# Attention of both layers: query rotation in two halves, per-head normalisation, ScalarE's high parts placed elsewhere, and the first tile's dense output products behind all groups

## The reference, cut to what matters

```python
q = (rmsnorm(cq, g_q[l]) @ w_uq[l]).reshape(B, S, 8, 64 + 32)
q_nope, q_rope = q[..., :64], apply_rope(q[..., 64:], cos_r, sin_r)   # the rotation
kv = (rmsnorm(ckv, g_kv[l]) @ w_ukv[l]).reshape(B, S, 8, 64 + 64)
o_a = mla_attention(q_nope, q_rope, k_nope, k_rope, v_mla)            # softmax, 8 heads
o_b = dsa_attention(...)                                              # 4 heads, 64 of the keys
o_c = silu(rg) * head_groupnorm(retention(...))
x = x + concatenate([o_a, o_b, o_c], axis=-1) @ w_out[l]              # dense output
hf = rmsnorm(x, g_mlp[l])
x = x + square(relu(hf @ w_ff1[l])) @ w_ff2[l]
```

## Time and profile before

| what | value |
|---|---|
| median of 3 runs | 1395.91 us (1393.72 to 1396.88) |
| profiled execution | 1395.43 us |
| its span | 1393.4 us |
| PE busy | 1347.1 us, 97% of the span |
| DVE, ACT, POOL busy | 622.7, 541.0, 449.3 us |
| TensorE clock | 9 in all 40 slices (full speed) |

### The profile page before, as it was taken

One profiled execution on the slowest core, in us unless ns is written; L12 is line 12 of the kernel. 1 busy time (PEld: TensorE's weight loads), 2 busy tenths in 40 slices (PEclk: granted clock), 3 DMA queues, 4 the chain that ended last, 5 costly groups with the idle time before them and its releaser, 6 DMA issues.

```text
span 1393.4 us, 19892 instructions
## 1 busy us (share of the span) xinstructions
PE 1347.1 (97%) x7754; PEld 931.0 (67%) x7754; DVE 622.7 (45%) x1060; ACT 541.0 (39%) x790; POOL 449.3 (32%) x295
## 2 busy tenths in 40 slices
PE   8998999999999999999999999999999999999998
PEld 7786788887887788888887877755434444344343
DVE  5685554544687455353344887523202112122021
ACT  6667644435576654343555562212111111111011
POOL 2384454444374544543867913000000000000000
PEclk9999999999999999999999999999999999999999
DMA  7441454553533355455786351479999999999997
GB/s 289 137 168 67 152 181 181 185 202 127 207 116 110 116 204 190 181 182 181 237 278 225 103 208 52 137 290 411 422 428 428 427 428 428 428 427 427 428 423 292
DMA packets 50250, 351.99 MB, mean 253 GB/s; under 512 B 7747, under 2 KB 9679, under 8 KB 25583
## 3 DMA queue, kind: packets, MB, share of 16 engines
q1 hardware_dynamic: 49438, 349.52, 64.9%
q10 hardware_dynamic: 720, 1.20, 0.2%
HBM read 347.78 MB, written 1.07 MB: 250 GB/s over the span
## 4 chain that ended last, share of the span: by engine, by line
PE 72%; DMA 11%; DVE 7%; ACT 3%; issue 3%; DVEq 2%; POOL 1%; SPq 0%; ACTq 0%; POOLq 0%
PE psum L1925 12%; PE psum L1101 9%; PE psum L1103 9%; PE psum L1102 9%; PE psum L1396 9%; DMA ring<-in_w_expert_up 8%; PE psum L1946 5%; PE psum L1398 4%; PE psum L1091 4%; PE psum L1853 2%; POOL weights_split L908 1%; PE psum L1863 1%; DMA arena<-in_w_expert_down 1%; DVE arena L2577 1%; ACT weights_split L2040 1%
## 5 line engine op out<-in xcount | busy, mean ns | idle before, releaser
L908 POOL TENSOR_TENSOR weights_split<-weights_raw,weights_split 128x512 fp32r<-128x512 f32 (+2 forms) x253 | 401.6, 1621 | 338.2 <-ACT weights_split L2040 338.2
L2040 ACT ACTIVATE weights_split<-weights_raw 128x2048 fp32r<-128x2048 f32 (+4 forms) x154 | 243.5, 1586 | 243.5 <-PE psum L1103 145.3
L1925 PE MATMUL psum<-ring,arena 128*64 128x512 f32 x944 | 226.5, 598 | 12.1 <-DMA ring<-in_w_expert_up 11.2
L1396 PE MATMUL psum<-h_split,weights_split 128*128 128x512 f32 x512 | 182.1, 399 | 3.1 <-DVE h_split L2028 2.7
L1925 PEld LDWEIGHTS psum<-ring,arena 128*64 128x64 f32 x944 | 73.4, 138 | 136.4 <-issue 135.8
L1101 PE MATMUL psum<-weights_split,h_split 128*128 128x512 f32 (+3 forms) x400 | 151.9, 380 | 4.3 <-POOL weights_split L908 2.4
L1101 PE MATMUL psum<-weights_split,hidden_split 128*128 128x512 f32 (+1 forms) x384 | 151.1, 393 | 4.3 <-DVE hidden_split L2028 4.3
L908 DVE TENSOR_TENSOR weights_split<-weights_raw,weights_split 128x2048 fp32r<-128x2048 f32 (+3 forms) x53 | 119.3, 2257 | 70.1 <-ACT weights_split L2040 68.3
L1102 PE MATMUL psum<-weights_split,h_split 128*128 128x512 f32 (+3 forms) x400 | 149.5, 374 | 0.0
L1103 PE MATMUL psum<-weights_split,h_split 128*128 128x512 f32 (+3 forms) x400 | 149.2, 373 | 0.0
L1103 PE MATMUL psum<-weights_split,hidden_split 128*128 128x512 f32 (+1 forms) x384 | 147.3, 384 | 0.0
(11 more groups left out here) (379 smaller groups left out, 1734.5 us busy)
## 6 DMA issues: line engine op xcount, KB each, us to landing
weights_raw<-in_layer_w SPq DMA_DIRECT2D x94, 1024.0 KB, 4.8
arena<-in_w_expert_down SPq DMA_DIRECT2D x28, 2048.0 KB, 14.7
ring<-in_w_expert_up SPq DMA_DIRECT2D x28, 2048.0 KB, 15.0
ring<-in_w_expert_gate SPq DMA_DIRECT2D x23, 2048.0 KB, 16.2
weights_raw<-in_second_w SPq DMA_DIRECT2D x44, 512.0 KB, 4.7
arena<-in_w_expert_gate SPq DMA_DIRECT2D x4, 2048.0 KB, 10.2
ring<-in_w_expert_up SPq DMA_DIRECT2D x8, 1024.0 KB, 13.1
arena<-in_w_expert_down SPq DMA_DIRECT2D x16, 512.0 KB, 12.3
```

The source lines that it names most:

```text
L908: ins = eng.tensor_tensor(W.part(j, 1, n)[:, cols], W.raw(j, n)[:, cols], W.part(j, 0, n).bitcast(F32)[:, cols], ALU.subtract)
L1396: pe.matmul(both.rearrange("p (w s) -> p w s", w=2), w[0][:, k, f * P:(f + 1) * P], hTp[:, :, k, :], start=(k == 0), stop=False)
L1925: ins = pe.matmul(bank[half(j), :], xe[h][:, k, half(j)], w[j][:, k, :], start=(k == 0), stop=(k == KD - 1))
L2040: act.activation(W.part(j, 0, w), W.raw(j, w), ACT.Copy).then_inc(W.hi, 1)
```

## The change

Four edits, in both layers.

1. VectorE rotates the queries in two calls, heads 0 to 3 behind `norm_probs(1)` and heads 4 to 7 behind `norm_probs(3)`, in place of one call behind `low_values(0)`. `low_values(0)` now stands behind them.
2. `norm_probs` multiplies head by head with `tensor_scalar` (two instructions for a group of two heads, four for one of four) in place of one `tensor_tensor` with a broadcast factor.
3. ScalarE makes the high part of out(1,1) in front of `exponentials(2)`, was behind the turned keys; that of out(0,0) behind the square root of the retention's variance, was behind `empty_turned(4)`; that of ff1(0,0) behind `high_values(7)`, was behind `high_values(6)`.
4. PE's dense output products: the chunks 4 and 5 come first and the wait for mixT stands in front of chunks 6 and 7; out(1,1) of tile 1 is cut in two, behind `turn_probs(7)` and `turn_probs(8)`; all products of piece out(0,0) and out(1,0) stand behind `attend_values(9)`. `add_out` follows them.

```diff
-                units.wait_emptied(("O", 0), ("mixT", 3))
-                project_out(0, 1, 0, range(4))
+                units.wait_emptied(("O", 0))
+                project_out(0, 1, 0, (0, 1))
                 units.wait_emptied(("O", 2))
-                project_out(0, 1, 1, range(4), True)
+                project_out(0, 1, 1, (0, 1))
+                units.wait_emptied(("mixT", 3))
+                project_out(0, 1, 0, (2, 3))
+                project_out(0, 1, 1, (2, 3), True)
...
                 attend_values(5)
-                project_out(1, 1, 1, range(4), True)
                 attend_mla(8)
                 turn_probs(7)
+                project_out(1, 1, 1, (0, 1))
                 attend_values(6)
+                attend_mla(9)
+                turn_probs(8)
+                project_out(1, 1, 1, (2, 3), True)
+                attend_values(7)
                 units.wait_emptied(("O", 4), ("O", 5))
-                project_out(0, 0, 0, (0, 1))
-                attend_mla(9)
-                project_out(0, 0, 0, (2, 3))
-                turn_probs(8)
-                attend_values(7)
-                project_out(1, 0, 0, range(4))
                 turn_probs(9)
                 attend_values(8)
+                attend_values(9)
+                project_out(0, 0, 0, range(4))
                 units.wait_emptied(("O", 6), ("O", 7))
                 project_out(0, 0, 1, (0, 1))
-                attend_values(9)
...
+                units.wait_emptied(("O", 8), ("O", 9))
+                project_out(0, 0, 1, (2, 3))
+                project_out(1, 0, 0, range(4))
                 units.wait_emptied(("wout", 0), ("wout", 1))
                 transposes(pe, units, "tr3", x, (0, 1))
-                project_out(1, 0, 1, (2, 3))
+                project_out(1, 0, 1, range(4))
...
                 empty_q(1)
+                split_after("uq", 0, 2)
                 exponentials(2)
...
                 act.activation(ret_rstd, ret_var, ACT.Sqrt, bias=eps_c, scale=1.0 / RET_E).then_inc(ret_std_ready.sem, 1)
+                split_after("ukv", 0, 0)
                 high_values(2)
...
                 high_values(7)
+                split_after("out", 1, 1)
                 empty_turned(9)
...
-                    rows = scores[g % 2][:, 0:n * nk].rearrange("p (h k) -> p h k", h=n)
-                    dve.tensor_tensor(rows, rows, rinv[g % 3][:, 0:n].unsqueeze(2).to_broadcast([P, n, nk]), ALU.mult).then_inc(probs_normed.sem, 1)
+                    for j in range(n):
+                        rows = scores[g % 2][:, j * nk:(j + 1) * nk]
+                        ins = dve.tensor_scalar(rows, rows, rinv[g % 3][:, j:j + 1], None, ALU.mult)
+                    ins.then_inc(probs_normed.sem, 1)
+
+                def rotate_queries(c):
+                    units.wait_emptied(("uq", T * c), ("uq", T * c + 1))
+                    return rotate(dve, *halves(q[:, :, 4 * c:4 * c + 4, NOPE:QK]), *angles(ROPE), q_tmp)
...
                 norm_probs(1)
+                rotate_queries(0)
...
                 norm_probs(3)
+                rotate_queries(1).then_inc(q_roped.sem, 1)
                 low_values(0)
-                units.wait_emptied(*(("uq", j) for j in range(2 * T)))
-                rotate(dve, *halves(q[:, :, :, NOPE:QK]), *angles(ROPE), q_tmp).then_inc(q_roped.sem, 1)
```

More of the change, by code:

```diff
@@ L344, in layer_plan @@
     plan += [scores[4], scores[5], ("mixT", 3, 7, "V"), turned[4], scores[6], turned[5], values[4], scores[7], turned[6], values[5], scores[8], turned[7], values[6], scores[9]]
-    plan += [wout[0], turned[8], values[7], wout[2], turned[9], values[8], values[9], wout[1]] + turned_x[:2] + [wout[3]] + turned_x[2:]
+    plan += [turned[8], values[7], turned[9], values[8], values[9], wout[0], wout[1], wout[2]] + turned_x[:2] + [wout[3]] + turned_x[2:]
     for b in range(FFB):
@@ L2180, in _ @@
                         dst, bank[0:NOPE, :].rearrange("p (c s) -> p c s", c=4), ACT.Copy), "A")
-                split_after("uq", 0, 2)
                 mix_gain = lambda k: gain(G_RET)(k - (KD - 2)) if k >= KD - 2 else None
@@ L2186, in _ @@
                 empty_turned(4)
-                split_after("ukv", 0, 0)
                 empty_turned(5)
@@ L2197, in _ @@
                 high_values(6)
-                split_after("out", 1, 1)
                 empty_turned(8)
@@ L2730, in _ @@
                 mask_scores(9)
-                add_out(0)
                 low_values(7)
                 norm_probs(9)
-                add_out(2)
                 low_values(8)
                 low_values(9)
+                add_out(0)
                 add_out(1)
+                add_out(2)
                 low_transposed(dve, units, "tr3", 2, gain(G_MLP), hTp, hT_hi, l, (0, 1), 1)
```

## The result

The changed kernel takes 1411.34 us (median of 3 runs, 1408.67 to 1412.46) against 1395.91: a ratio of 1.0108, 95% interval 1.0085 to 1.0131. It is slower, and by more than the forecast range allowed. The profiled execution took 1408.67 us, 13.2 more than that of before, and its span is 1406.6 us. In that trace the last feed-forward matmul of layer 0 starts 5.3 us later than before, that of layer 1 12.9 us later, and the rest of the program adds 0.3. It leaves out the rest of the program, which no edit touches and which took 750.8 to 757.8 us in the fourteen traces. But each shift is read from one trace, and no run shows by how much it varies from execution to execution.

What follows compares the result with a forecast made beforehand. It took PE, busy 97% at full clock, as the bound, with only idle time to win. Losses at retO(1) and in the loop, less removed waits, gave +3.9 us per layer, +7.8 in all: 1403.5 us, range 1393.5 to 1408.5.

Steps and rivals of the forecast that it cites:

- What bounds the kernel: Whole kernel: PE is busy 97% at full clock, so only its idle time can be won; four waits, 5.7 us.
- Turn-taking of VectorE and GpSimd: Normalisation and rotation before retO(1): each such VectorE instruction costs one GpSimd step, 1.3 us; PE's scores +3.7 us.
- one grant: Rival at retO(1): two VectorE instructions pass between GpSimd steps, +1.9 instead of +3.7 us; total 1399.9 us, chance 0.15.
- no hold: Rival: GpSimd doesn't hold the new VectorE instructions, retO(1) costs +0.2 us; total 1394.2 us, chance 0.15.
- Rotated queries: Start of the turned queries: the 1.33 us wait goes, PE begins at 112.46 us, +2.4 us.
- ScalarE's high part, L2703 and L2706: Retention: out(0,0) delays scores(4) by 0.45 us, its low part holds these lines, +1.0; retention turned +3.9 us late.
- Chunks first: At turn(4): chunks 4 and 5 cover the whole 2.2 us wait for the low part of mixT; lateness falls to +1.6 us.
- Group 6: At turn(6): the 1.2 us wait for the normalisation goes, turn(6) at 132.66 us, +0.3 us.
- The loop: MLA groups: the 4.1 us chain is no longer covered, PE idles 5.5 us; last dense product +4.8 us late.
- Into the feed-forward part: Behind tr3: four chunks cover the 0.9 us wait, leaving +3.9 us for the layer, with nothing taking it back.
- The shorter TENSOR_SCALAR: Head-by-head norm: almost no gain counted; by the skill's rule each of three turns some 0.2 us shorter, total 1.2 less.
- The sum: Whole kernel: 2 layers x 3.9 = +7.8 us, 1403.2 or 1403.7 us; 1403.5 taken, chance 0.5 with its neighbours.

Runs made afterwards that it cites:

- the busy waits: The changed kernel with unneeded matmuls in front of three PE waits (scores of groups 2 and 3, turn_probs(7), turn_probs(9)): 1405.01 us.
- the kernel before with a longer wait: The kernel before with six unneeded VectorE additions in front of the rotation, to lengthen PE's wait for the rotated queries: 1408.24 us.
- without GpSimd's steps: The changed kernel with GpSimd making the low part of out(0,1) for 16 columns only instead of 2048: 1402.85 us.
- the later runs: The unchanged kernel before, run on the same chip beside the first eight follow-up kernels: 1397.3 us.
- The parts: The kernel before with one part each: chunks first 1396.92, loop's order 1409.76, rotation in halves 1405.68, tensor_scalar for each head 1403.54, high parts 1402.35 us.
- the loop alone: The kernel before with only the loop's new order of dense products, add_out, PSUM bank order and high part of ff1(0,0): 1409.76 us.

## Why the prediction was wrong

The direction was right and so were the waits, most of them within 0.3 us. What failed is their price: the sum had no term for TensorE's clock, and the range missed the time by 2.8 us. Point by point:

- **What bounds the kernel.** Here lies the step that failed: "its clock stands at 9 in every slice, so only PE's idle time can be won". The page's row is too coarse to show it, and a clock that stood through the attention's waits of at most 2.2 us was carried over to a kernel with waits of 2.4 and 3.0 us. So the sum priced each microsecond of idle time at one and the fall of the clock at nothing. The runs put the clock at 4.1 us of the change's 12.9: the busy waits won just that, and in the kernel before with a longer wait 6.1 us came with the clock on top of the added wait. No rival had it either.
- **Turn-taking of VectorE and GpSimd**: right. Norm 0 and 1 took 1.89 and 2.33 us, the rotation's first three 1.37, 1.35 and 1.22, and without GpSimd's steps 0.29. retO(1) was forecast for 103.9 us, measured 103.46; the scores 104.0 against 103.52. The rivals of one grant and of no hold are both refuted by these rows.
- **Rotated queries**: the wait for L2456 is gone, as forecast, but the turned queries begin at 113.4 us, not 112.46. The difference is the clock behind the scores: with the waits kept busy they begin at 112.33.
- **ScalarE's high part, L2703 and L2706**: forecast waits 0.45 and 1.0 us, measured 0.4 and 0.8.
- **Chunks first**: the 2.2 us wait is gone; alone it is worth 1.3 us in layer 0 and 2.1 in layer 1, 3.4 in all, and the sum had 1.6 for a layer.
- **Group 6**: its wait is gone. turn(6) was forecast at 132.66 and came at 134.03, with the waits kept busy at 132.78.
- **The loop**: waits forecast 3.1, 0.8 and 1.6 us, measured 3.03, 0.55 and 1.61. The period is 4.25 us (139.32 to 143.57 to 147.82), not 4.1. By estimate from these rows that is 0.3 us for each layer.
- **Into the feed-forward part**: 0.9 us were to be won and nothing taken back. The right size is luck. There were two waits for L2028, 1.3 us in all, of which the earlier trace rows has the longer one, and both are gone; but the wait for L908 grew by 0.5 and 0.3 us in the two layers.
- **The shorter TENSOR_SCALAR.** By the rule of the Trainium skill ("VectorE: DVE Perf Modes", The TRN2 errata) each turn would by estimate have been 0.2 us shorter than my 4.1; it was 0.15 longer. The measurement decides: the pair takes 0.6 us.
- **The sum**: 2 x 3.9 = 7.8 forecast; 4.1 + 4.7 = 8.8 measured at full clock, 12.9 with the clock as granted. The difference of the medians (15.4) is another 2 us above that of the profiled runs (13.2). Taken against the kernel before in the later runs (1397.3) it is 14.0, so part of this rest is in the three runs of before. I have no trace of the other two runs of the changed kernel, and their mean clock (0.991) is lower than that of the profiled run (0.992) by no more than the last digit. What is left of it stays open.

The parts don't add up: -3.4, +12.0, +9.5, +7.1 and +3.5 make 28.7 us, and together they cost 12.9. A large part is the clock: the four parts that lose have ten half-speed stretches of 3.4 us in the layers of their traces, and all edits together have 13.7 us, as much as four of these. By estimate at half speed that is up to 17 us against up to 6.8. Two overlaps show in the rows besides. The rotation has to wait for ScalarE until 96.97 us anyway, so the slower norms in front of it cost nothing more there. And with the high parts moved GpSimd is away from norm 6, whose pair takes 0.62 us in the changed kernel where it took 2.58 alone. How much of the rest each makes isn't shown.

## What to carry to other kernels

Before dense work is moved out of a loop of dependent small steps, take the period of that chain from the trace (here 4.1 to 4.25 us from turn to turn) and check that what stays covers it. Before one element-wise instruction of VectorE is cut into several, or moved, look at what GpSimd runs at that time: each new instruction with two SBUF inputs, and each TENSOR_SCALAR within SBUF, costs up to a whole GpSimd step (1.3 us here) while there is one. And price a wait of TensorE of some microseconds with what its clock does behind it, read from windows of a few microseconds and not from the page's slices; a few unneeded matmuls in the wait show in one run whether the clock has a part in the loss.

## What the runs showed of the hardware

- Behind single waits of 2.2 to 4.3 us TensorE ran 3.4 or 6.8 us at half its clock (0.50 of 2.4 GHz): eight matmuls took 2.08 us in place of 1.13. Not each such wait had this effect: of the two waits of 3.03 us for turn(7) in the changed kernel only the second layer's had, and the wait of 2.2 us for mixT had it in both layers of the kernel with the longer wait, in one layer of the loop alone and in none of the kernel before. The Trainium skill, "TensorE: Matmul & The Clock Gate", HAM oscillation, says that idle time between bursts of matmuls lets the clock fall; the traces agree.
- Matmuls whose result nobody reads kept the clock at 1.00 through waits of the same length, and were worth 4.1 and 5.2 us in the shift.
- Of VectorE instructions queued one behind the other each gave way to the next GpSimd step: four TENSOR_SCALAR of 128x128 in a row took 1.89 and 2.33 us by pairs, where four of the same size took 0.89 us together while GpSimd was idle (norm 4 of the changed kernel). A RECIPROCAL of two elements between them took 0.15 us and was not held.
